# Second attention of a two-block kernel: scores by blocks of keys, no transposes, sums of exponentials added on VectorE and GpSimd

## The reference, cut to what matters

```python
def gqa_attention(q, k, v, q_norm, k_norm):      # 8 query heads, 2 key heads, 64 wide
    q = apply_axial_rope(rms_norm(q, q_norm)); k = apply_axial_rope(rms_norm(k, k_norm))
    scores = einsum('bqhgd,bkhd->bhgqk', q_blk, k) / sqrt(64)   # q_blk: 128 queries
    p = softmax(scores, axis=-1)                                 # over all 1024 keys
    return einsum('bhgqk,bkhd->bqhgd', p, v)
```

## Time and profile before

| | |
|---|---|
| median of 3 runs | 2559.88 us (2558.03 to 2565.32) |
| profiled execution | 2559.82 us, its span 2558.0 us |
| TensorE busy | 96% of the span |
| VectorE, ScalarE, GpSimd busy | 65%, 44%, 36% |
| `gqa` in the profiled execution | 1605.3 to 1816.8 us |

### The profile page before, as it was taken

How to read it: one execution, slowest core, us unless ns; L and a number is a source line. 1 busy time by engine, 2 the same in 40 slices (tenths; PEclk the granted TensorE clock), 3 DMA queues, 4 the chain that set the end, 5 groups by cost and what they waited for, 6 DMA issues and landing times.

```text
span 2558.0 us, 33358 instructions
## 1 busy us (share of the span) xinstructions
PE 2445.4 (96%) x12995; PEld 1972.4 (77%) x12995; DVE 1671.9 (65%) x2252; ACT 1128.8 (44%) x1867; POOL 916.6 (36%) x627
## 2 busy tenths in 40 slices
PE   8999997988879999999999999899999999999997
PEld 6788885658868788888888787666687888888885
...
DMA packets 136284, 300.64 MB, mean 118 GB/s; under 512 B 30272, under 2 KB 30656, under 8 KB 136000
## 3 DMA queue, kind: packets, MB, share of 16 engines
...
## 4 chain that ended last, share of the span: by engine, by line
PE 74%; DVE 12%; ACT 6%; POOL 4%; issue 2%; DMA 2%; SPq 1%; DVEq 0%; ACTq 0%; POOLq 0%
PE ps L381 20%; PE ps L382 20%; PE ps L383 20%; ACT t L397 4%; PE ps L1004 2%; PE ps L988 2%; PE ps L1024 2%; POOL t L2822 1%; DVE t L670 1%; DMA t<-g_d 1%; POOL t L2830 1%; ACT t L398 1%; DVE t L731 1%; ACT t L1087 1%; DVE t L1138 1%
## 5 line engine op out<-in xcount | busy, mean ns | idle before, releaser
L397 ACT ACTIVATE t<-t 128x512 fp32r<-128x512 f32 (+6 forms) x1136 | 759.6, 706 | 1110.3 <-PE ps L383 663.5
L381 PE MATMUL ps<-t 128*128 128x512 f32 (+1 forms) x2778 | 1090.2, 392 | 27.5 <-DVE t L650 7.7
L383 PE MATMUL ps<-t 128*128 128x512 f32 (+1 forms) x2778 | 1082.9, 390 | 0.0
L382 PE MATMUL ps<-t 128*128 128x512 f32 (+1 forms) x2778 | 1082.7, 390 | 0.0
L381 PEld LDWEIGHTS ps<-t 128*128 128x128 f32 x2778 | 524.5, 189 | 145.8 <-issue 17.5
L382 PEld LDWEIGHTS ps<-t 128*128 128x128 f32 x2778 | 524.6, 189 | 109.5 <-issue 2.6
L383 PEld LDWEIGHTS ps<-t 128*128 128x128 f32 x2778 | 524.3, 189 | 108.8
L2822 POOL TENSOR_TENSOR t<-t 128x512 fp32r<-128x512 f32 x280 | 416.9, 1493 | 356.0 <-ACT t L397 356.0
L484 POOL TENSOR_TENSOR t<-t 128x1024 fp32r<-128x1024 f32 x80 | 199.6, 2498 | 523.3 <-ACT t L397 523.3
L2550 DVE TENSOR_TENSOR t<-ps,t 128x512 f32<-128x512 f32 x200 | 136.8, 686 | 202.5 <-PE ps L383 202.5
L397 ACT ACTIVATE t<-ps 128x512 f32<-128x512 f32 (+5 forms) x330 | 165.9, 530 | 122.5 <-PE ps L1658 33.8
...
## 6 DMA issues: line engine op xcount, KB each, us to landing
...
```

What stands on the lines that cost most here:

```text
L381: e.matmul(out, ah, bh, start=start, stop=False, skip_group_check=goes_on)
L382: e.matmul(out, ah, bl, start=False, stop=False, skip_group_check=goes_on)
L383: return e.matmul(out, al, bh, start=False, stop=stop, skip_group_check=goes_on)
L397: return e.activation(out, in_, fn, scale=scale)
```

## The change

The attention is rebuilt around *units* (512 queries of one tile c, 8 of them) and *places* (one block of 128 keys of one unit, 64 of them, x = 8u + k):
- scores are made with keys as weights and queries as columns, so they come out as keys by queries, as the values product needs them; the transposes and both copies are gone. `PT` now holds 512 queries for each head;
- the maximum over keys lies across rows then, so a coarse score (high parts alone, queries by keys) is made only for it (`pe_top`), VectorE reduces it (`dve_top`), TensorE turns the negated maxima into a row (`rows`), ScalarE copies the row into a zeroed tile `M`, and one more product, ones by `M`, adds it to the scores. The exponentials (two of 512 columns a place) need no bias then;
- the coarse scores of unit 0 are made and reduced inside the Fourier part of `mix2`; those of later units stand between the score products of earlier places (`tops_at`);
- sums of exponentials: GpSimd adds the seven later blocks for head 1 and the first three for head 0, VectorE the last four for head 0; a product with ones sums over rows; ScalarE makes the reciprocal by logarithm and exponential, VectorE refines it in two steps and multiplies;
- the values of place x - 2 follow the scores of place x;
- the norm steps of c = 1 start six steps ahead of place 0 and all are spread one step a place (`NORM_PLACES`); `pool_spread` of group g moves to place 8g + 6; SP issues the raw loads for c = 2 and 3 between the stores of the Fourier result.

The core of the diff, of which removed lines are shown only where they are short (they are in the listing above):

```diff
-        Q_.PT = [[sb(st, [128, 8, 256]) for _ in range(2)] for _ in range(2)]
+        Q_.PT = [sb(st, [128, 8, 512]) for _ in range(2)]
...
         Q_.Q += [tuple(sb(st, [128, L], R) for _ in range(2))]
...
-        Q_.P = [[sb(st, [128, L]) for _ in range(2)], [B_.raw[W_OUT2 % NR], B_.raw[(W_OUT2 + 1) % NR]]]
+        Q_.acc = [[sb(st, [128, 512]) for _ in range(2)] for _ in range(2)]
         Q_.raw = sb(st, [128, L])
-        Q_.diag = sb(st, [128, 2, 4, 128])
-        Q_.nmx = [sb(st, [128, 2]) for _ in range(4)]
-        Q_.sums, Q_.parts = sb(st, [128, 16]), sb(st, [128, 16])
+        Q_.M = [sb(st, [128, 512], R) for _ in range(2)]
+        Q_.ones = sb(st, [128, 128], R)
+        Q_.tops, Q_.negs = sb(st, [128, 16]), [sb(st, [128, 8]) for _ in range(2)]
     keep.close()
     B2 = Tiles()
     with ExitStack() as st:
...
+                if 2 * g + x >= 2:
+                    pe_top(e, w, 2 * g + x - 2)
+        pe_top(e, w, 6)
+        pe_top(e, w, 7)
...
+                if 2 * g + x >= 2:
+                    dve_top(e, w, 2 * g + x - 2)
+        dve_top(e, w, 6)
+        dve_top(e, w, 7)
...
+    top_slot = slot(1)
+    tops_g, scores_g, aside_g = ring([top_slot]), ring([ps[:, i, :] for i in range(4, 8)]), ring([ps[:, 0, :]])
+    o_g = ps[:, 1, :]
+    UNITS_G, PLACES_G = 8, 64
+    steps_g = range(-6, PLACES_G + 10)
+    added = lambda j, x: (gq_add_p if j else gq_add_h if x % 8 < 4 else gq_add, x)
+    half_of = lambda u: halves[u % 2]
...
+    def tops_at(x):
+        if x == 12:
+            return [20, 21]
+        if x == 13:
+            return [22, 23]
+        y = x + 8 if 8 <= x < 12 else x + 10
+        return [y] if 8 <= y < PLACES_G and not 6 <= x < 8 else []
...
+            self.places = banks if self.early else scores_g
...
+            return [pe_slot(w, (what, self.c, h), until, self.places) for h in range(2)]
...
+    NORM_PLACES = [0, 2, 3, 4, 5, 6, 7, 8, 10, 12, 13]
...
+                at = x - (16 * c - 26 if c > 1 else -6)
+                if at in NORM_PLACES:
+                    norm(e, w, later[c], NORM_PLACES.index(at))
...
+    def pe_top(e, w, y):
+        u, t, k = y // 8, y % 8 // 2, halves[y % 2]
+        if u == 0:
+            places = [pe_slot(w, ("top", y, j), [(gq_top, y)], banks) for j in range(2)]
+        else:
+            p = pe_slot(w, ("top", y), [(gq_top, y)], tops_g)
+            places = [p[:, h] for h in halves]
+        w.wait_ge(q_hi, "k")
+        w.wait_ge(q_hi, u // 2)
+        for j in range(2):
+            r = rows_of(j)
+            m = e.matmul(places[j], Q_.Q[u // 2 % 2][0][r, tok[4 * (u % 2) + t]], Q_.KV[0][r, k], start=True, stop=True)
+        m.then_inc(*gq_max.up(y))
+    def dve_top(e, w, y):
+        u, at = y // 8, 8 * (y % 2) + y % 8 // 2 * 2
+        w.wait_ge(gq_max, y)
+        if u == 0:
+            for j in range(2):
+                m = e.tensor_reduce(Q_.tops[:, at + j:at + j + 1], banks["top", y, j], AX, MAX, negate=True)
+        else:
+            m = e.tensor_reduce(Q_.tops[:, at:at + 2], top_slot.rearrange("p (j n) -> p j n", j=2), AX, MAX, negate=True)
+        m.then_inc(*gq_top.up(y))
+        if y % 8 == 7:
+            w.wait_ge(gq_top, y)
+            if u >= 2:
+                w.wait_ge(gq_rows, u - 2)
+            e.tensor_tensor(Q_.negs[u % 2][:], Q_.tops[:, 0:8], Q_.tops[:, 8:16], ALU.min).then_inc(*gq_neg.up(u))
     def pe_gqa(e, w):
...
+        between = norms_between(e, w, pe_norm)
+        tops_g.until[0] = banks.until[2] + banks.until[3]
+        scores_g.until[:] = [banks.until[i] for i in range(4, 8)]
+        aside_g.until[0] = banks.until[0]
         before_o = banks.until[1]
...
+        def rows(u):
+            p = pe_slot(w, ("rows", u), [(gq_row, u)], aside_g)
+            w.wait_ge(gq_neg, u)
+            for t in range(4):
+                for j in range(2):
+                    m = e.matmul(p[64 * j:64 * j + 1, tok[t]], Q_.negs[u % 2][:, 2 * t + j:2 * t + j + 1], IDENT,
+                                 start=True, stop=True)
+            m.then_inc(*gq_rows.up(u))
+        def scores(x, tops):
+            u, k = x // 8, tok[x % 8]
+            (qh, ql), (kh, kl), q = Q_.Q[u // 2 % 2], Q_.KV, half_of(u)
+            places = [pe_slot(w, (x, j), [(gq_exp, (x, j))], scores_g) for j in range(2)]
+            w.wait_ge(q_lo, "k")
+            w.wait_ge(q_lo, u // 2)
+            for i, (kk, qq) in enumerate(((kh, qh), (kh, ql), (kl, qh))):
+                for j in range(2):
+                    r = rows_of(j)
+                    e.matmul(places[j], kk[r, k], qq[r, q], start=i == 0, stop=False)
+            for y in tops:
+                pe_top(e, w, y)
+            w.wait_ge(gq_row, u)
+            for j in range(2):
+                r = rows_of(j)
+                e.matmul(places[j], Q_.ones[r, :], Q_.M[u % 2][r, :], start=False, stop=True).then_inc(*gq_score.up((x, j)))
+        def values(x):
+            u, k = divmod(x, 8)
+            if k == 0 and u:
+                w.wait_ge(gq_o, u - 1)
+            w.wait_ge(v_copy, 1)
+            V = Q_.V[:].rearrange("p (t n) -> p t n", t=8)
+            for j in range(2):
+                w.wait_ge(gq_exp, (x, j))
+            for j in range(2):
+                m = e.matmul(o_g[rows_of(j), :], V[:, k, rows_of(j)], Q_.PT[j][:, k, :], start=k == 0, stop=k == 7)
+            m.then_inc(*gq_value.up(x))
+        def sums(u):
+            p = pe_slot(w, ("sums", u), [(gq_f0, u)], aside_g)
+            for j in range(2):
+                w.wait_ge(*added(j, 8 * u + 7))
+            for j in range(2):
+                m = e.matmul(p[rows_of(j), :], ONES[:, 0:64], Q_.acc[j][u % 2][:], start=True, stop=True)
+            m.then_inc(*gq_sum.up(u))
+        for s, k in before_o:
+            w.wait_ge(s, k)
+        w.wait_ge(z_csl, (3, 1))
+        for g in range(4):
+            m = e.matmul(o_g[:, g:g + 1], AW[:, tok[g]], M_.ny[:, g:g + 1], start=True, stop=True)
+        m.then_inc(*z_ny.up(0))
+        rows(0)
+        for x in steps_g:
+            tops = tops_at(x)
+            if 0 <= x < PLACES_G:
+                scores(x, tops[0:1])
+            else:
+                for y in tops[0:1]:
+                    pe_top(e, w, y)
+            between(x)
+            if 0 <= x - 2 < PLACES_G:
+                values(x - 2)
+            for y in tops[1:]:
+                pe_top(e, w, y)
+            u, at = divmod(x, 8)
+            if at == 6 and 0 <= u < UNITS_G - 1:
+                rows(u + 1)
+            if at == 2 and 0 <= u - 1 < UNITS_G:
+                sums(u - 1)
     def act_gqa(e, w):
...
+        between = norms_between(e, w, act_norm)
+        def row_copies(u):
+            w.wait_ge(gq_rows, u)
+            if u >= 2:
+                w.wait_ge(gq_score, (8 * u - 9, 1))
+            for j in range(2):
+                r = slice(64 * j, 64 * j + 1)
+                m = act(e, Q_.M[u % 2][r, :], aside_g["rows", u][r, :], ACT.Copy)
+            m.then_inc(*gq_row.up(u))
+        def exps(x):
+            u, k = divmod(x, 8)
+            for j in range(2):
+                if u:
+                    w.wait_ge(gq_value, x - 8)
+                    w.wait_ge(*added(j, x - 8 if k else x - 7))
+                w.wait_ge(gq_score, (x, j))
+                act(e, Q_.PT[j][:, k, :], scores_g[x, j], ACT.Exp).then_inc(*gq_exp.up((x, j)))
+        act(e, Q_.ones[:], ONES, ACT.Copy)
+        w.wait_ge(rope_load[0], 0)
+        for M in Q_.M:
+            m = act(e, M[:], cos[:, 0:512], ACT.Copy, scale=0.0)
+        m.then_inc(*gq_zero.up(0))
+        w.wait_ge(gq_zero, 0)
+        w.wait_ge(z_ny, 0)
+        act(e, M_.ny_out[:], o_g[:, 0:4], ACT.Copy).then_inc(*z_nyr.up(0))
+        row_copies(0)
+        for x in steps_g:
+            u, at = divmod(x, 8)
+            if at == 2 and 0 <= u - 1 < UNITS_G:
+                w.wait_ge(gq_value, 8 * u - 1)
+                act(e, B_.gq[:, (u - 1) // 2, half_of(u - 1)], o_g, ACT.Copy).then_inc(*gq_o.up(u - 1))
+            if at == 7 and 0 <= u < UNITS_G - 1:
+                row_copies(u + 1)
+            if 0 <= x < PLACES_G:
+                exps(x)
+            if at == 4 and 0 <= u - 1 < UNITS_G:
+                v = u - 1
+                if v == 0:
+                    w.wait_ge(q2_store[2], (1, 9))
+                else:
+                    w.wait_ge(gq_out, v - 1)
+                w.wait_ge(gq_sum, v)
+                act(e, Q_.scale[:], aside_g["sums", v], ACT.Ln).then_inc(*gq_ln.up(v))
+                w.wait_ge(gq_ln, v)
+                act(e, Q_.scale[:], Q_.scale[:], ACT.Exp, scale=-1.0).then_inc(*gq_r0.up(v))
+            between(x)
+    def add_up(e, w, x, j):
+        u, k = divmod(x, 8)
+        if k == 0:
+            return
+        acc, P = Q_.acc[j][u % 2][:], Q_.PT[j]
+        if k == 1 and u >= 2:
+            w.wait_ge(*((gq_sum, u - 2) if j else (gq_f1, u - 2)))
+        if k > 1:
+            w.wait_ge(*added(j, x - 1))
+        done, _ = added(j, x)
```

(39 more changed lines are left out.)

59 lines of the change are left out of this document (7 added, 52 removed).

## The result

| | before | changed |
|---|---|---|
| median of the timed runs | 2559.74 us | 2586.16 us |
| lowest to highest | 2558.03 to 2565.32 us (4 runs) | 2583.41 to 2586.77 us (4 runs) |
| span of the profiled execution | 2558.0 us | 2581.6 us |
| mean granted clock of TensorE | 0.978 | 0.970 |

The ratio of the runs is 1.010, with a 95% interval from 1.0086 to 1.0114. The kernel became 26 us slower. The prediction was 2563.0 us, with a range from 2544 to 2579, so the time lies 7 us above the range, on the side of rival B.

What follows compares the result with a forecast made beforehand. TensorE was taken as the bound (busy 96%). First scores 1621.7 + cold clock 1.5 + loop 173.3 + stalls 15.9 + tail 7.5 = 1819.9 against 1816.7, +3.2 us: 2563.0 us, range 2544 to 2579.

Steps and rivals of the forecast that it cites:

- rival B: Attention loop: VectorE and GpSimd set the pace, stalls grow by 10 to 16 us, 2573 to 2579 us; chance 0.24.
- the one on the queue: SP's loads for c = 2, 3 against its stores: claimed to cost nothing; some 3 us if the cover failed.
- the stalls of VectorE: Attention loop: TensorE waits for VectorE's maxima in crowded places, notably 12 to 16; 15.9 us in all.
- fits, barely: GpSimd beside the loop: adds, norm steps and spread take 20.8 us a unit against 23.3 for TensorE.
- the change of shape: TensorE in the loop: each change of product shape costs 0.16 to 0.21 us, 128 changes before and after.
- the row products: TensorE in the loop: seven blocks turning maxima into rows, 1.4 us each (bounds 0.9 and 1.9), 9.8 us.
- the last b product: End of the Fourier stage: ends at 1611.9 instead of 1605.3, the stage 6.6 us longer with unit 0's maxima.
- The start behind it: From last b product to first scores: chain over three engines, 9.8 us, plus 1.5 for the lower clock.
- The tail: From the end of the last scores to VectorE's last step of the attention: 7.5 us.
- the 16.4 us called waits: Attention of the kernel before: what its 211.5 us hold beyond 195.1 of priced work, most at the start.
- A: Attention loop: the side engines fit, stalls 6 us instead of 15.9, row products 1.1; 2551 us; chance 0.31.
- C: First norm and first places: the cold start lasts, clock stays at 1.2 GHz, 6 us more, 2569; chance 0.08.

Runs made afterwards that it cites:

- e1: Changed kernel with SP's raw load of query tile 2 issued ahead of the store of Fourier group 0; 2572.93 us, 1.0045 of the kernel before.
- e2: Changed kernel with all four spreads at the start of GpSimd's part, SP's order kept; 2575.76 us, 1.0055 of the kernel before.
- e15: e8 with SP's order put back as in the changed kernel; 2566.06 us, 1.0021 of the kernel before.
- e7: e1 with query tile 1's square ahead of ScalarE's zeroing and row copies, its sum product ahead of the row products; 2566.26 us, 1.0027 of the kernel before.
- e3: e2 with GpSimd's adds nearly taken away (eight of ten on one column, first adding ones; sums not the reference's); 2557.31 us, 0.9983 of the kernel before.
- e4: e2 with all seven adds of head 0 on VectorE, GpSimd keeping head 1's; 2571.73 us, 1.0043 of the kernel before.
- e8: e1 with the edit of e5, the edit of e7 and finishing steps split over places 5, 6, 7; 2553.17 us, 0.9977 of the kernel before.
- e11: e8 with the thin GpSimd adds of e3 (sums not the reference's); 2547.8 us, 0.9954 of the kernel before.
- e5: e1 with VectorE's adds of head 0 two places later and the sums one place later; 2567.64 us, 1.0030 of the kernel before.

## Why the prediction was wrong, point by point

**The step that failed** is the one on the queue: "*SP:* the raw loads for c = 2, 3 stand ahead of the stores of mixed rows; both are wanted tens of us later. Nothing. If this cover failed, a square would wait some 3 us." The code has it otherwise: the load for c = 2 stands behind the first store, and that for c = 3 behind the second. I looked at when the loads and the stores were wanted, and not at what they wait for in SP's order. So one load stands behind a store whose data the change itself makes some 35 us later. The load left SP at 1651.01, where it could have left near 1634 (in e1 and e2 it leaves 9.3 us behind the first scores). Place 8 began at 1646.58, and the terms of the forecast put it near 1646.5; that it fits so well is luck, as the first scores came 1.6 us late and the eight places took 21.8 us where the forecast gives 23.3. Place 9 should have begun some 4.3 us later and began 18.6 us later. Of the 14.3 us lost, e1 shows 7.8 to be the load (its place 8 takes 10.7 us), and e15, where little else holds that place up, 11.6. By the medians the order costs 13 us (e1) or 11 us (e15). The 6.4 us that are still lost in e1 are 3.2 of waiting for the high part and about as much from the lower clock behind it (3.78 us of sum products against 1.98 in e7, and longer coarse and value products). They go when anything ahead of the high part gets shorter or earlier: thin adds (e3, place 8 takes 4.9 us), all adds of head 0 on VectorE (e4, 5.7), or the norm begun earlier (e7, 5.7).

**The term that was too small** is the stalls of VectorE (15.9 us), by some 5 us in places 24 to 40. From place 8 to 24 the changed kernel needed 69.3 us where the forecast gives 55; all of that difference is place 8. From 24 to 32 it needed 27.5 instead of 25.8, from 32 to 40 28.4 instead of 24.8, and from 40 to 48 21.8 as forecast. GpSimd "fits, barely" is wrong in units 2 and 4, where norm steps and adds stand in one order and VectorE's add, which has to continue GpSimd's sum, starts the moment GpSimd's ends (1708.7 and 1762.9). I named the contention by the Trainium skill ("GPSIMD Engine Reference", Specifications), and it is there: 0.97 against 0.79 for the add, 0.99 against 0.69 for a finishing step, in the changed kernel and in e3. But the length of the stretched work alone doesn't set the price: the adds cost 18.5 us in e2, and 5.9 us once VectorE's order is looser (e8 against e11), though VectorE's adds are no shorter there (1.07 us) and its load is the same (2.6 us a place from 9 to 40 in both kernels). What differs is how much TensorE waits for it: 6.0 us for the first finishing step of a unit (L3543) in the changed kernel and 0.5 in e8, 9.6 and 6.8 for the coarse maxima. How much of the 18.5 us is stretching and how much is the late start of VectorE's adds isn't shown; in two places of the loop VectorE's add starts as GpSimd's ends, and there VectorE is busy with a stretched instruction until then.

**Right** were the prices of TensorE: 2.36 and 2.13 us a place against 2.38 and 2.15, so the change of shape costs what the kernel before showed, with only four value records between. The values block is 1.01 (1.02 forecast), the sums 0.86, and the row products, 0.97, were below my 1.4 and inside the bounds; that alone gave 3 us back. Near, if late, was the last b product, which ended at 1613.7 (1611.9 forecast), behind a wait of 2.1 us for a maximum and 3.2 us at a clock of 0.50 (1606.0 to 1609.2); a maximum of 512 took 0.68 and not 0.61. The start behind it took 11.1 us (9.8 + 1.5 forecast), so the first scores began at 1624.8 (1621.7 + 1.5). From place 48 to 63 it took 36.1 us against 36.8. The tail from the end of the last scores is 8.6 us, forecast 7.5: VectorE's last adds are stretched there as well (1.78, 1.82 and 0.70 us).

**Slips in the working**, none of which changes the verdict: of the 16.4 us called waits TensorE was idle for 13.5, 6.2 of them at the start; coarse products stand in 52 places of the loop, two of which hold two, not in 54; the parts of the tail make 7.0 us, not 7.5; and rival B's own parts make 29 to 30 us of VectorE a unit (8 x 1.22, six or seven instructions of 1.3, 10.9), not 28.3.

**The rivals.** B had the right sign and the right engines, and 2573 to 2579 is about what e1 and e2 measured (2572.9 and 2575.8), the changed kernel without the fault on SP. Its mechanism was half right. VectorE's instructions are stretched, and its mean load did pass B's mark of 2.38 us a place: 39.7 us in places 9 to 23 and 42.1 in 24 to 39 are 2.6 a place. But that is 21 us a unit and not 28, below TensorE's own work with norms, sums and rows (43.3 us in places 9 to 23, 2.9 a place), and e8 carries the same load with far fewer stalls. Crowded single places set them. A named 2551 us, and e8 came to 2553 by edits that loosen the order, not by the engines missing each other as A had it. C did not come on its own: at the start the mean clock was 0.85 and 0.92 of full, and in place 8 it fell within the 11.9 us wait.

**Open** stays how the 18.5 us of GpSimd's adds divide into stretching and late starts, and whether e5 gains by its slack behind GpSimd or by emptying place 5. A kernel with VectorE's adds two places later and GpSimd's adds made thin one head at a time, or with another step moved out of place 5 instead of the add, would tell.
